# Two-block hybrid kernel: NSA loop pieces 8/6/5/5, compression in paired rows, 128x4 post-norm statistics

## The chip, the cores and the metric

One core of one Trainium2 chip runs the whole program. The metric is the time of one execution in device microseconds; the runs shown are three executions of the same kernel. An engine's name is short here: PE is TensorE, DVE is VectorE, ACT is ScalarE, POOL is GpSimd, SP is SyncE.

## What is computed

The reference runs two layers, one after the other, on one sequence of 512 tokens with 1024 channels, in fp32. Only what the change touches is told in detail.

- **First block.** RMS norm, an input projection `h @ w_in`, then NSA attention (8 query heads in 2 groups, head width 64), an RWKV-7 scan, a gated merge, an output projection and a convolutional FFN, each with a residual.
- Within NSA three attentions share the queries: one over compressed keys, one over selected blocks, one over a window. **Compression** takes blocks of 32 rows of 64 channels at a stride of 16 (31 blocks), adds a position term and multiplies by `w1`:

```python
blocks = z.reshape(B, S, G, Dh)[:, tok] + pe[None, None, :, None, :]
hid = jax.nn.silu(jnp.einsum('bnlgd,lde->bnge', blocks, w1))
return jnp.einsum('bnge,ef->bgnf', hid, w2)
```

- **Second block.** SwiGLU FFN, a mixer (dilated-window attention and a chunkwise mLSTM, with sigmoid gates), and a second SwiGLU FFN. Each of the three results goes through an RMS norm of its own before it is added to `x`; these are the three **post norms**:

```python
x = x + 0.5 * rmsnorm(f, ffn1_post_g[l])
x = x + rmsnorm(y, mix_post_g[l])
x = x + 0.5 * rmsnorm(f, ffn2_post_g[l])
```

- The mLSTM needs running sums and running maxima of its input and forget gates over time, one row of 512 per head (`b = cumsum(log f)`, and the running maximum of `i - b`).

## The kernel before

Activations lie with channels on the 128 partitions and the 512 tokens along the free axis. A **unit** is one 128-column block of a weight matrix against all 1024 channels: eight k-steps. fp32 weights and activations are split into a rounded high part and a low rest, so a unit is 24 matmuls of 128x512: high by high and low by high (`mm_hi`, 16), then high by low part of the weights (`mm_lo`, 8). All of them are recorded at L379, and `unit` is the helper that issues them. For each unit SP loads `raw` (512 KB), ACT rounds it to `w_hi` (`high_part`, L1117) as soon as the unit two before has been used, POOL makes `w_lo` in two instructions (L352), PE works, and DVE takes the PSUM bank out with the norm factor (`take`, L1599). Weights and the two PSUM banks of the units alternate between two slots. The order of the work on every engine is written out by hand; engines meet in counted semaphores.

**Compression** (PE L460 to 467). DVE adds the position term into `blocks` in four instructions of 128x496 (L1654), two for keys (`c` = 0, from `u[4]`) and two for values (`c` = 1, from `u[5]`), with the takes of units 6 and 7 between them. PE then runs, for 32 rows `l`, 2 tensors and 2 groups, a matmul with 64 contracted rows, 64 weight columns and 31 moving columns; both groups have their own bank (`p7`, `p6`). fp32 matmuls show up as two instructions each. ACT applies Silu in four instructions (L1170, L1172). Unit 8 follows on PE. The weights `cmp_w1` come by one DMA of 2 MB, written twice, once for either half of the partitions.

**The NSA loop** (PE from L621, 16 turns). Turn `t` handles query block `b = t % 4` of head pair `t // 4`, and its attention grows with `b`: the scores are 128(b+1) wide. On PE a turn is `nsa_turn(t, 0)` (transposes of the exponentiated scores of group 0), `loop_part`, `nsa_back(t-1)` (transpose of the last turn's output, which waits for `nsa_mix`), `nsa_turn(t, 1)`, `nsa_scores(t+1)`, `loop_part`, `nsa_pv(t)` (128x65 matmuls). `nsa_turn(t, 1)` waits until ACT and DVE (`slc_copy`, `win_copy`, L1220 and L1764) have emptied the banks of group 0. The two `loop_part` calls of a turn carry one dense unit of the RWKV and merge projection, four k-steps each, in bank `p0`. Three units stand in four turns; the turn with `t % 4 == 0` has none:

```python
if t % 4 == 0:
    return
w = loop_unit(t)
```

DVE's turn is `win_copy` twice, `nsa_max(t+1)` (L1748), the take of the unit (L1805), `nsa_mix(t)` (L1771 to L1778, waits for `nsa_pv(t)`) and `mix_previous(t-1)` (L1788). ACT's is `slc_copy`, `nsa_store`, `slc_copy`, `nsa_exp(t+1)`, the `high_part` of the unit two ahead, `scale_part`.

**Post norms.** `f_tiles` (L2150) squares and sums eight tiles into `acc` (128x512). `stat_of_acc` (L430) sums over the partitions with an all-ones 128x128 weight into `p2`, so every partition holds all 512 sums; `stat_root` (L1127) takes the square root on 128x512; DVE takes the reciprocal in place in `p3` (L1615); `post_scale` (L2169) multiplies the eight stored tiles by `p3`, POOL (or DVE, in every other tile of the last norm) adds them to `x` and the next stage begins. This stands behind `down2`, `out2` and `down3`.

**Gate rows of the mLSTM.** DVE computes them on 4x512: `gate_sums` (L2199 to L2205, with a scan) behind column block 2, and `gate_maxima` (L2210 to L2214, with a scan) behind column block 3 of attention head 0. Column blocks 0 to 5 of a head are also rotated on DVE (`rope_it`, L2236 to L2247), and block 8 is the last before the attention steps, in which `att_max` (L2255) is DVE's next work.

## Time and profile before

| what | us |
|---|---|
| three runs | 2529.43, 2523.91, 2526.45 |
| median | 2526.45 |
| the profiled execution | 2526.31 |
| its span, first to last instruction | 2524.4 |
| mean granted TensorE clock, share of full speed | 0.974 |
| busy: PE / DVE / ACT / POOL | 2410.1 / 1050.1 / 959.8 / 1045.0 |

A unit has 24 matmuls; where PE has nothing else to do units follow each other every 5.44 us. In the chain of work that ended last PE has 86% of the span and DVE 9%. PE's busy time overlaps itself in places (a matmul's end is modelled), so it says when PE had no work, not how well it worked. In a timeline a row holds several equal instructions in a row (x8), its length is from the first start to the last end, and the bracket tells how long the engine had been idle and who ended that. "issue" is idle time with no releaser in the profile.

### The profile page before, as it was taken

The page shows a single profiled execution, that of the slowest core. Times are in us where ns is not written, and L with a number is a line of the kernel's source. Part 1 is how long each engine was busy: PE and PEld are TensorE (multiplying, and loading weights), DVE is VectorE, ACT ScalarE, POOL GpSimd, SP SyncE. Part 2 cuts the span into 40 slices and gives each one's busy share as a digit, 9 for nine tenths or more (in the row PEclk, how much of TensorE's full clock was granted, in tenths as well). Part 3 has the DMA queues.
Part 4 walks back from the last instruction along what each step waited for, and adds up shares of the span by engine and source line. Part 5 has one row for each costly group of instructions (what it writes and reads, how often), then busy time and mean ns, then how long its engine had stood idle before and what let it go on. Part 6 is the DMA issues. An engine that isn't in the chain of part 4 may idle for free.

```text
span 2524.4 us, 38784 instructions
## 1 busy us (share of the span) xinstructions
PE 2410.1 (95%) x13928; PEld 1953.1 (77%) x13928; DVE 1050.1 (42%) x1776; ACT 959.8 (38%) x1273; POOL 1045.0 (41%) x756
## 2 busy tenths in 40 slices
PE   8999998889999999999999799999999998999997
PEld 6877777767788888788887578787888775888885
DVE  3355464555555532322211856663333345322213
ACT  3244432233566643444422422223444523444321
POOL 4212230014445555555555533442433255455554
PEclk9899999989999999999999899999999998999998
DMA  4111120013232233222332212221222132223232
GB/s 171 58 42 38 46 71 16 3 42 110 82 100 99 92 101 107 92 95 96 100 100 100 96 59 76 84 78 65 76 82 78 64 100 67 85 98 100 93 107 83
DMA packets 56746, 205.24 MB, mean 81 GB/s; under 512 B 6828, under 2 KB 7596, under 8 KB 56268
## 3 DMA queue, kind: packets, MB, share of 16 engines
q1 hardware_dynamic: 55152, 196.45, 23.6%
q10 hardware_dynamic: 1504, 7.49, 0.8%
q8 instruction: 70, 1.15, 0.2%
q14 instruction: 20, 0.16, 0.0%
HBM read 201.81 MB, written 2.10 MB: 81 GB/s over the span
## 4 chain that ended last, share of the span: by engine, by line
PE 86%; DVE 9%; ACT 2%; issue 2%; POOL 0%; DMA 0%; DVEq 0%; ACTq 0%; SPq 0%
PE psum L379 84%; DVE rope_t L2245 2%; DVE qk_st L2244 1%; PE psum L554 1%; DVE rope_t L2237 1%; DVE qk_st L2247 1%; POOL x L364 0%; PE psum L978 0%; DVE psum L1615 0%; ACT w_hi L1117 0%; DVE inv L1934 0%; DVE o_acc L1778 0%; DVE rst L1615 0%; DVE soft_r L1773 0%; DVE tmp L2169 0%
## 5 line engine op out<-in xcount | busy, mean ns | idle before, releaser
L352 POOL TENSOR_TENSOR w_lo<-raw,w_hi 128x512 fp32r<-128x512 f32 x732 | 1014.6, 1407 | 1447.8 <-ACT w_hi L1117 1447.8
L379 PE MATMUL psum<-h_hi,w_hi 128*128 128x512 f32 x2192 | 890.6, 406 | 40.8 <-DVE h_lo L1621 26.0
L379 PE MATMUL psum<-h_lo,w_hi 128*128 128x512 f32 x2192 | 865.4, 395 | 0.0
L1117 ACT ACTIVATE w_hi<-raw 128x1024 fp32r<-128x1024 f32 x366 | 386.2, 1056 | 807.7 <-PE psum L379 796.8
L379 PE MATMUL psum<-h_hi,w_lo 128*128 128x512 f32 x2192 | 551.9, 391 | 0.0
L379 PEld LDWEIGHTS psum<-h_hi,w_hi 128*128 128x128 f32 x2192 | 419.0, 191 | 153.1 <-issue 54.2
L379 PEld LDWEIGHTS psum<-h_lo,w_hi 128*128 128x128 f32 x2192 | 419.5, 191 | 89.3 <-issue 6.9
L379 PEld LDWEIGHTS psum<-h_hi,w_lo 128*128 128x128 f32 x2192 | 412.8, 188 | 87.5 <-issue 1.4
L379 PE MATMUL psum<-hid_hi,w_hi 128*128 128x512 f32 x528 | 208.7, 395 | 0.0
L379 PE MATMUL psum<-hid_lo,w_hi 128*128 128x512 f32 x528 | 208.6, 395 | 0.0
L1599 DVE TENSOR_TENSOR tmp<-psum,rst 128x512 f32<-128x512 f32 x100 | 69.1, 691 | 319.5 <-PE psum L379 319.0
L379 PE MATMUL psum<-hid_hi,w_lo 128*128 128x512 f32 x528 | 134.9, 395 | 0.0
L2159 DVE TENSOR_TENSOR acc<-acc,sq 128x512 f32<-128x512 f32 x24 | 30.8, 1283 | 242.7 <-ACT sq L1403 242.7
L379 PEld LDWEIGHTS psum<-hid_hi,w_hi 128*128 128x128 f32 x528 | 99.1, 188 | 24.3 <-DVE tmp L2132 0.2
L379 PEld LDWEIGHTS psum<-hid_lo,w_hi 128*128 128x128 f32 x528 | 99.2, 188 | 24.0
L379 PEld LDWEIGHTS psum<-hid_hi,w_lo 128*128 128x128 f32 x528 | 99.1, 188 | 24.0
L2143 DVE TENSOR_TENSOR hid_lo<-tmp,hid_hi 128x512 f32 x66 | 50.9, 771 | 62.5 <-ACT hid_hi L1452 62.5
L1448 ACT ACTIVATE tmp<-tmp 128x512 f32<-128x512 f32 x44 | 27.8, 632 | 113.7 <-DVE tmp L1599 113.7
L1452 ACT ACTIVATE hid_hi<-tmp 128x512 f32 x66 | 41.7, 632 | 72.4 <-DVE tmp L2141 72.4
L2128 DVE SCALAR_TENSOR_TENSOR tmp<-psum,par,tmp 128x511 f32<-128x511 f32 x44 | 33.0, 750 | 71.1 <-ACT tmp L1440 71.1
L1448 ACT ACT_TABLE_LOAD x44 | 56.5, 1283 | 0.8
L1604 DVE TENSOR_TENSOR psum<-psum,rst 128x512 f32<-128x512 f32 x60 | 41.6, 694 | 35.6 <-PE psum L379 35.4
(391 smaller groups left out, 2533.5 us busy)
## 6 DMA issues: line engine op xcount, KB each, us to landing
raw<-in_w SPq DMA_DIRECT2D x366, 512.0 KB, 3.3
x<-in_x SPq DMA_DIRECT2D x4, 512.0 KB, 6.3
tmp<-in_cmp_w ACTq DMA_DIRECT2D x1, 2048.0 KB, 7.3
x<-in_x ACTq DMA_DIRECT2D x1, 2048.0 KB, 7.7
out_y<-x SPq DMA_DIRECT2D x8, 256.0 KB, 2.1
mask<-in_mask ACTq DMA_DIRECT2D x1, 1536.0 KB
masks<-in_masks ACTq DMA_DIRECT2D x1, 768.0 KB, 9.4
lora<-in_lora ACTq DMA_DIRECT2D x1, 512.0 KB, 3.7
```

The lines of the kernel that those rows point to most:

```text
L352: pool.tensor_tensor(w_lo[:, g.slot, part], raw[:, g.slot, part], w_hi[:, g.slot, part].bitcast(F32), ALU.subtract).then_inc(sem("lo_ready ...
L379: return pe.matmul(out, lhsT, rhs, start=start, stop=stop)
L554: last = pe.transpose(psum[:, 6 + r, tok(m)], att_s[t % 2][2 * g + r][:, tok(m)], ident[:])
L1117: act.activation(w_hi[:, g.slot], raw[:, g.slot], ACT.Copy).then_inc(sem("hi_ready"), 1)
L1448: act.activation(tmp[:, 2], tmp[:, 4], ACT.Silu).then_inc(sem("silu_done"), 1)
L1452: act.activation(tile_of(hid_hi, i), tmp[:, 3], ACT.Copy).then_inc(sem("hid_rounded"), 1)
L1599: dve.tensor_tensor(dst, psum[:, o.slot], rst[:], ALU.mult).then_inc(sem(f"freed{o.slot}"), 1)
L1604: dve.tensor_tensor(psum[:, o.slot], psum[:, o.slot], rst[:], ALU.mult)\
L2128: dve.scalar_tensor_tensor(tmp[:, c, 1:], psum[:, ob.slot, 0:T - 1], col("ffn_conv", 2 * KF + c + 2 * i), tmp[:, c, 1:], ALU.mult, ALU.add ...
L2143: dve.tensor_tensor(tile_of(hid_lo, i), tmp[:, 3], tile_of(hid_hi, i).bitcast(F32), ALU.subtract)\
L2159: dve.tensor_tensor(acc[:], acc[:], sq[:, ob.slot], ALU.add).then_inc(sem("acc_done"), 1)
L2245: dve.tensor_tensor(t, t, sin, ALU.mult).then_inc(sem("rope_a"), 1)
```

## The change

- **NSA loop.** Pieces of units no longer follow `t`: the four turns of a group carry 8, 6, 5 and 5 k-steps (all of unit 0 in turn 0; 3 and 3 k-steps of unit 1 in turn 1; the last 2 of unit 1 and the first 3 of unit 2 in turn 2; 3 and 2 of unit 2 in turn 3). Units end in turns 0, 2 and 3; the take on DVE and `high_part` on ACT follow them, in turn 2 the take stands between the two `win_copy`.
- **Compression.** Two rows (`l` even and odd) lie on the two halves of the partitions, and both groups side by side as moving columns. PE: 16 x 2 matmuls with 128 contracted rows, 64 weight columns and 62 moving columns into one bank. DVE: 16 additions of 64x248 in place of 4 of 128x496, eight before the take of unit 6 and eight behind it; the take of unit 7 now follows `blocks_ready`. ACT: three Silu. The weights come in two DMAs of 64 partitions, 1 MB in all, in runs of 64 elements.
- **Post norms.** PE multiplies `acc` as weights by one column of ones, four times, into 128x4 (token by partition); ACT's root and DVE's reciprocal work on 128x4; PE spreads the result with four matmuls against `ident` into `p3`.
- **Gate rows.** `gate_sums` goes behind column block 8 of head 0, `gate_maxima` behind that of head 1, the rest (`gate_floor`) behind that of head 2; the exponential on ACT moves from head 1 to head 3. `b_row` has another place in memory.

The diff, cut to what matters:

```diff
-        def loop_unit(t):
-            return Index(A_UNITS + 4 + 3 * (t // 4) + t % 4 - 1)
+        LOOP_PIECES = (((0, 0, 4), (0, 4, 8)), ((1, 0, 3), (1, 3, 6)), ((1, 6, 8), (2, 0, 3)), ((2, 3, 6), (2, 6, 8)))
+        def loop_unit(t, n):
+            return Index(A_UNITS + 4 + 3 * (t // 4) + n)
+        def unit_ended(t):
+            return (0, None, 1, 2)[t % 4]
...
+            def post_stat(a, r):
+                pe.wait_ge(sem("acc_done"), 9 * a + 9)
+                for b in range(TB):
+                    last = mm(p2[:, b:b + 1], acc[:, tok(b)], sel[:, 2:3])
+                last.then_inc(sem("stat_sum"), 1)
+                pe.wait_ge(sem("stat_rstd"), r + 1)
+                for b in range(TB):
+                    last = mm(p3[:, tok(b)], stat4[:, 1, b:b + 1].to_broadcast([128, 128]), ident[:])
+                last.then_inc(sem("stat_spread"), 1)
...
-            for l in range(32):
+            for l in range(16):
                 for c in range(2):
-                    for g in range(NG):
-                        last = mm((p7, p6)[g][half(c), 0:NC], cmp_w1[half(g), c, l],
-                                  blocks[half(g), c, l, 0:NC], l == 0, l == 31)
+                    last = mm(hidden[half(c)], cmp_w1[:, c, l], row_pairs[:, c, l], l == 0, l == 15)
...
-            def loop_part(t, ks):
-                if t % 4 == 0:
-                    return
-                w = loop_unit(t)
+            def loop_part(t, piece):
+                n, first, end = LOOP_PIECES[t % 4][piece]
+                w, ks = loop_unit(t, n), range(first, end)
...
+            def post_root(r):
+                act.wait_ge(sem("stat_sum"), r + 1)
+                act.activation(stat4[:, 0], p2[:, 0:TB], ACT.Sqrt, bias=eps, scale=1.0 / D).then_inc(sem("stat_root"), 1)
...
-            act.dma_start(cmp_w1, io["cmp_w1"]).then_inc(sem("cmp_in"), 16)
+            for n in range(2):
+                act.dma_start(cmp_w1[half(n)], io["cmp_w1"][half(n)].rearrange("p c (l n) e -> p c n l e", n=2)[:, :, n])\
+                    .then_inc(sem("cmp_in"), 16)
...
-                if t % 4:
-                    high_part(loop_unit(t) + 2)
+                if t % 4 != 1:
+                    high_part(loop_unit(t, unit_ended(t)) + 2)
...
+            def post_rstd(r, n):
+                dve.wait_ge(sem("stat_root"), r + 1)
+                dve.reciprocal(stat4[:, 1], stat4[:, 0]).then_inc(sem("stat_rstd"), 1)
+                dve.wait_ge(sem("stat_spread"), n)
...
             for c in range(2):
-                src = u[:, 4 + c].rearrange("p (n s) -> p s n", s=16)
-                for m in range(2):
-                    last = dve.tensor_tensor(
-                        blocks[:, c, 16 * m:16 * m + 16, 0:NC], src[:, :, m:m + NC],
-                        cmp_pe[:, c, 16 * m:16 * m + 16].unsqueeze(2).to_broadcast([128, 16, NC]), ALU.add)
-                    if m == 0:
-                        take_u(6 + c)
+                src = u[:, 4 + c].rearrange("p (n l a) -> p a l n", l=8, a=2)
+                add = cmp_pe[:, c].rearrange("p (l a) -> p a l", a=2)
+                for a in range(2):
+                    for g in range(NG):
+                        for m in range(2):
+                            last = dve.tensor_tensor(
+                                row_pairs[half(a), c, 8 * m:8 * m + 8, g], src[half(g), a, :, m:m + NC],
+                                add[half(g), a, 8 * m:8 * m + 8].unsqueeze(2).to_broadcast([64, 8, NC]), ALU.add)
+                if c == 0:
+                    take_u(6)
             last.then_inc(sem("blocks_ready"), 1)
+            take_u(7)
...
             for t in range(16):
                 win_copy(t, 0)
+                if t % 4 == 2:
+                    take_loop(t)
                 win_copy(t, 1)
...
-                        if hh == 0 and c == 2:
-                            gate_sums()
-                        if hh == 0 and c == 3:
-                            gate_maxima()
                         if c == 7:
                             att_max(0)
+                        if c == 8 and hh < 3:
+                            (gate_sums, gate_maxima, gate_floor)[hh]()
```

## Rows read from the trace of the kernel before

**Rows 1.** The page: engines over the whole span (busy us, share, instructions)
```profile
PE 2410.1 (95%) x13928; PEld 1953.1 (77%) x13928; DVE 1050.1 (42%) x1776; ACT 959.8 (38%) x1273; POOL 1045.0 (41%) x756
```

**Rows 2.** Windows of the NSA loop: stretch, length, busy (x instructions), clock, DMA
```profile
135.20:173.70 38.50, 36.51 (x228) 29.63 (x229) 20.56 (x72) 18.15 (x33) 8.68 (x7) 1.00 0.12 42
173.70:216.50 42.80, 39.94 (x231) 31.85 (x230) 24.35 (x79) 19.06 (x35) 7.54 (x7) 0.92 0.11 38
216.50:302.60 86.10, 81.32 (x450) 65.09 (x449) 44.97 (x148) 35.82 (x65) 16.11 (x13) 0.88 0.11 37
```

**Rows 3.** Windows around turn 0 of the second group
```profile
173.60:181.80 8.20, 5.94 (x28) 4.43 (x28) 5.57 (x25) 3.12 (x8) 0.43 (x1) 0.70 0.19 65
176.60:183.90 7.30, 6.93 (x27) 5.50 (x27) 4.50 (x19) 3.23 (x7) 0.00 (x0) 0.53 0.04 16
```

**Rows 4.** Timeline of PE in turn 2, second group: start, length, instruction, idle before
```profile
192.67 0.48 PE L379 MATMUL psum<-h_hi,w_hi 128*128 128x512 f32 x1
...
196.19 0.85 PE L554 MATMUL psum<-ident,tmp 128*128 128x128 f32 x6 [0.43 <-DVE blocks L1764]
```

**Rows 5.** Timeline of DVE in the same turn
```profile
192.29 0.18 DVE L1771 RECIPROCAL soft_r<-psum 128x4 f32<-128x4 f32 x1 [1.04 <-PE psum L379]
192.51 1.29 DVE L1773 TENSOR_TENSOR soft_r<-soft_r,gate_tm 128x4 f32<-128x4 f32 x1
...
195.51 0.54 DVE L1764 COPY blocks<-psum 128x384 f32<-128x384 f32 x1
```

**Rows 6.** Windows over the compression matmuls and the unit behind them
```profile
63.90:70.70 6.80, 6.76 (x256) 6.76 (x256) 1.00 (x1) 1.22 (x1) 2.20 (x2) 0.53 0.31 96
70.70:78.30 7.60, 7.60 (x29) 6.13 (x27) 0.00 (x0) 0.70 (x4) 0.00 (x0) 0.75 0.01 2
```

**Rows 7.** By tile: DVE's additions into `blocks`, duration ns min/median/max
```profile
L1654 DVE TENSOR_TENSOR blocks<-u,cmp_pe x4: 993/1022/2001, 52.1 to 62.8; 128x496 f32<-128x496 f32 x4
```

**Rows 8.** Timelines of POOL, DVE and PE around them
```profile
52.51 3.01 POOL L352 TENSOR_TENSOR w_lo<-raw,w_hi 128x512 fp32r<-128x512 f32 x2 [2.90 <-ACT w_hi L1117]
...
57.36 2.94 DVE L1654 TENSOR_TENSOR blocks<-u,cmp_pe 128x496 f32<-128x496 f32 x2
...
57.95 3.46 POOL L352 TENSOR_TENSOR w_lo<-raw,w_hi 128x512 fp32r<-128x512 f32 x2 [2.43 <-ACT w_hi L1117]
...
63.94 6.86 PE L379 MATMUL psum<-blocks,tmp 64*64 64x31 f32 x256 [1.78 <-DVE blocks L1654]
```

**Rows 9.** Timeline of PE: fp32 matmuls of other shapes
```profile
111.21 1.97 PE L379 MATMUL psum<-ident,rq 128*64 128x128 f32 x32
...
1481.19 1.50 PE L379 MATMUL psum<-v_tm,att_pT 128*128 128x129 f32 x12
```

**Rows 10.** Timeline behind the last down-projection tile of the first SwiGLU FFN
```profile
1391.18 1.20 PE L379 MATMUL psum<-acc,sel 128*128 128x512 f32 x2 [3.04 <-DVE acc L2159]
1392.42 0.66 ACT L1127 ACTIVATE psum<-psum,sel 128x512 f32<-128x512 f32 x1 [1.39 <-PE psum L379]
...
1393.11 3.37 DVE L1615 RECIPROCAL psum<-psum 128x512 f32<-128x512 f32 x1 [1.32 <-ACT psum L1127]
...
1396.51 1.88 DVE L2169 TENSOR_TENSOR tmp<-tmp,psum 128x512 f32<-128x512 f32 x3
```

**Rows 11.** Timeline of ACT: a small square root
```profile
81.99 0.29 ACT L1178 ACTIVATE rq<-psum,sel 128x32 f32<-128x32 f32 x1 [0.73 <-PE psum L379]
```

**Rows 12.** Attention head 0: timelines of DVE and PE
```profile
1439.06 2.19 DVE L2202 TENSOR_TENSOR_SCAN tmp<-tmp 4x512 f32<-4x512 f32 x1
...
1477.98 0.69 DVE L2255 CUSTOM_DVE_ANT_0 att_p<-psum,mask 128x512 f32<-128x512 f32 x1 [2.64 <-issue]
...
1443.64 0.47 PE L379 MATMUL psum<-h_hi,w_hi 128*128 128x512 f32 x1 [0.76 <-DVE qk_st L1599]
...
1453.63 0.77 PE L379 MATMUL psum<-h_hi,w_hi 128*128 128x512 f32 x1 [4.30 <-DVE qk_st L2283]
```

**Rows 13.** Window of the unit behind PE's longest wait there
```profile
1453.60:1460.90 7.30, 7.27 (x25) 5.95 (x26) 6.86 (x11) 0.00 (x0) 0.00 (x0) 0.77 0.22 74
```

More of the change, by code:

```diff
@@ L250, in build_program @@
         selh = sb("selh", [4, 128], scope=ml)
-        rows, b_row, zero_row = tmp[0:4, 0:4], tmp[0:4, 6], tmp[0:4, 7]
+        rows, b_row, zero_row = tmp[0:4, 0:4], mo[0:4, 4], tmp[0:4, 7]
         c_row, em_row, nmu_row = mo[0:4, 5], mo[0:4, 6], mo[0:4, 7]
@@ L605, in _ @@
                 nsa_turn(t, 0)
-                loop_part(t, range(0, 4))
+                loop_part(t, 0)
                 if t:
@@ L611, in _ @@
                     nsa_scores(t + 1)
-                loop_part(t, range(4, 8))
+                loop_part(t, 1)
                 nsa_pv(t)
@@ L1104, in _ @@
                     unit(Index(FIRST["out2"] + c, i, 2), Index(254 + c, i, 2), y2_hi, y2_lo, ("y_ready", 8))
-            stat_of_acc(3)
+            post_stat(3, 5)
             ffn_mm(2, 6, "up3", "down3", 262)
-            stat_of_acc(4)
+            post_stat(4, 7)
         @block.scalar
@@ L1168, in _ @@
             act.wait_ge(sem("gain_ready"), 1)
-            for g, bank in enumerate((p7, p6)):
-                act.activation(hid_cmp[:, g, 0:NC], bank[half(0), 0:NC], ACT.Silu)
-            for g, bank in enumerate((p7, p6)):
+            act.activation(hid_cmp[:, :, 0:NC], hidden[half(0)], ACT.Silu)
+            for g in range(NG):
                 last = act.activation(hid_rep[half(1), g, :, 0:NC],
-                                      bank[half(1), 0:NC].unsqueeze(1).to_broadcast([64, 4, NC]), ACT.Silu)
+                                      hidden[half(1), g].unsqueeze(1).to_broadcast([64, 4, NC]), ACT.Silu)
             last.then_inc(sem("cmp_act"), 1)
@@ L1499, in _ @@
                         high_part(gu + c)
-                        if hh == 1 and c == 0:
+                        if hh == 3 and c == 0:
                             act.wait_ge(sem("row_v"), 6)
@@ L1610, in low_h, with rms_rstd @@
                     .then_inc(sem("h_ready"), 1)
-            def rms_rstd(r, dst=rst[:]):
+            def rms_rstd(r):
                 dve.wait_ge(sem("stat_root"), r + 1)
-                dve.reciprocal(dst, p3).then_inc(sem("stat_rstd"), 1)
+                dve.reciprocal(rst[:], p3).then_inc(sem("stat_rstd"), 1)
                 dve.wait_ge(sem("stat_rstd"), r + 1)
+            def post_rstd(r, n):
+                dve.wait_ge(sem("stat_root"), r + 1)
+                dve.reciprocal(stat4[:, 1], stat4[:, 0]).then_inc(sem("stat_rstd"), 1)
+                dve.wait_ge(sem("stat_spread"), n)
             def low_x(nset, gains, k):
@@ L1651, in _ @@
             for c in range(2):
-                src = u[:, 4 + c].rearrange("p (n s) -> p s n", s=16)
-                for m in range(2):
-                    last = dve.tensor_tensor(
-                        blocks[:, c, 16 * m:16 * m + 16, 0:NC], src[:, :, m:m + NC],
-                        cmp_pe[:, c, 16 * m:16 * m + 16].unsqueeze(2).to_broadcast([128, 16, NC]), ALU.add)
-                    if m == 0:
-                        take_u(6 + c)
+                src = u[:, 4 + c].rearrange("p (n l a) -> p a l n", l=8, a=2)
+                add = cmp_pe[:, c].rearrange("p (l a) -> p a l", a=2)
+                for a in range(2):
+                    for g in range(NG):
+                        for m in range(2):
[4 more added lines that the diff above has]
+                    take_u(6)
             last.then_inc(sem("blocks_ready"), 1)
+            take_u(7)
             dve.tensor_scalar(gain[:, 0:3], par[:, COL["qk_gain"] + 1:COL["qk_gain"] + 4],
@@ L1796, in _, with take_loop @@
             cmp_out(3)
+            def take_loop(t):
+                w = loop_unit(t, unit_ended(t))
+                dve.wait_ge(sem("unit_used"), w.value(1))
+                dve.tensor_tensor(zm[:, w.at - A_UNITS, 1:], p0, rst[:], ALU.mult).then_inc(sem(f"freed{w.slot}"), 1)
             for t in range(16):
                 win_copy(t, 0)
+                if t % 4 == 2:
+                    take_loop(t)
                 win_copy(t, 1)
```

29 lines of the change are left out of this document (15 added, 14 removed).

## The prediction

> **What bounds the kernel now.** I read the page first, then windows over the stages, then the timelines of PE and DVE where the change falls. PE has work in 95% of the span [rows 1], so only three things can give time back: PE's idle time, time at the lower of its two clock levels (1.2 instead of 2.4 GHz), and PE instructions that go away. For each edit the reader is to look for these three at its place. The profiled execution took 2526.3 us, its span is 2524.4; the sum below is made against 2526.3, and the median of the runs, 2526.45, is the same within 0.2 us.
>
> **NSA loop.** The loop is four groups of four turns. The first takes 38.5 us at granted clock 1.00 with PE busy 36.5 us; the second takes 42.8 at 0.92, the last two 86.1 at 0.88, so 128.9 for three, 43.0 each [rows 2]. The difference sits in turn 0, which has no dense piece: in 8.2 us around it PE is busy 5.94, so 2.3 us idle, and from there it runs 7.3 us at clock 0.53 [rows 3], which costs 7.3 x (1 - 0.53) = 3.4 us. Together 5.7 us. The change puts a whole unit, 8 k-steps, into that place, so both go. It adds two piece starts per group (8 pieces for 6, some 0.15 us each as PE's first matmul of a piece is longer, 0.48 against 0.39: 0.3 in all), hence work of 36.8 us.
>
> What is late next is DVE. Behind a turn's `nsa_pv` it must do `nsa_mix`, `mix_previous` and `win_copy` before PE may start the second transposes. In turn 2 of the second group this ran from 192.1 (DVE's wait ended at 192.29) to 196.19, 4.1 us, against which PE had a piece of four k-steps (12 matmuls, 2.7 us, from 192.67) and still waited 0.43 us [rows 4, 5]. Of the 4.1 us some 1.1 is one 4-column operation that took 1.29 us where the reciprocal of the same size took 0.18 [rows 5]; POOL is then at work on the unit just rounded. After the change that piece has 3, 2, 3 k-steps in turns 1, 2, 3, so 0.7, 1.4 and 0.7 us less cover; in turn 2 the stall goes (no unit ends in turn 1, POOL has nothing), and in turn 1 it comes (unit 0 now ends in turn 0). I take waits of 1.1, 0.7 and 0.5 us, and none in turn 0, where four k-steps lie before the transposes: 2.3 us a group. Bounds: 0.8 if POOL is never in the way, 4.0 if always. A group is then 36.8 + 2.3 = 39.1 us, and the three lose 128.9 - 117.3 = **11.6 us** (16.7 to 6.5). The first group, at full clock already, stays at its 38.5. The take in turn 2, now between the two copies, costs 0.7 us of DVE while PE has transposes and scores: nothing. The `high_part` on ACT behind turn 0 stands behind `nsa_exp`, and `slc_copy` of the next turn only has to be there a piece later: nothing. Each unit's weights are still rounded one whole unit ahead, and SP's loads move with them; POOL, which frees `raw` for them, is busy 41% [rows 1].
>
> **Compression.** PE: 256 instructions took 6.86 us at clock 0.53 [rows 6, 8], with four 64x64 tiles side by side; now 64 with two. An instruction of two tiles with 128 moving columns took 1.97/32 = 0.062 us at full clock [rows 9]; so 64 cost 3.9 us, or at most double, 7.9, if the clock is low, as it was in the unit behind a wait of 4.30 us [rows 12, 13] and will be after the wait below. With half the columns I take 5.8 us: 1.0 saved. The Trainium skill's "TensorEngine Tiling (Array Packing)", section Instruction Overhead, says that a matmul has an overhead of about 60 cycles and that one column costs as much as 60. By that page the rounds count, 64 before and 32 now, and 6.86 would become an estimated 3.4 us; no row here shows it.
>
> DVE: an addition of 496 columns took 0.99 us when alone and 2.00 when POOL was at work [rows 7, 8]; POOL's own pair, 2.5 us of work, took 3.01 and 3.46 beside them [rows 8]. So they take turns, whole instruction by whole instruction. An addition has now half the columns, 0.55 us, and there are 16: 8.8 us for 4.0 of before, on half the partitions each, so nothing is gained by their height. From 52.1: eight additions (4.4), the take of unit 6 (0.7), eight more (4.4) end at 61.8 with no wait, when PE finishes unit 7 (62.2); PE began at 63.94, so the gain would be 1.7. But each POOL pair that meets them puts two instructions of about 1.25 us between them. The pairs start at 52.5 and 57.95 [rows 8] and one unit, 5.4 us, later at 63.4; the first two push the end to about 66.8, so the third is met too, and it becomes 69.2. PE would start at 69.3, **5.4 us later**. The skill's "SBUF — State Buffer" (on the shared GPSIMD/Vector port) calls it an exclusive lock held for the whole instruction, not a split of bandwidth. By sharing instead of a lock the three pairs would cost half, some 3.7 us, and PE would start near 65.5; the 2.00 beside 0.99 speaks for the lock. I take the lock: +5.4 - 1.0 = **+4.4 us**, bounds -6.5 (no wait, 1.7; matmuls at 3.9 us, 3.0; no low clock in unit 8, which cost 7.6 x 0.25 = 1.9 [rows 6]) and +7. The take of unit 7 has 5 us until unit 9 needs its bank. Two DMAs in runs of 256 bytes are issued 27 us before they are needed; ACT's queue had over 3 us to spare before the next rounding. Nothing for both.
>
> **Post norms.** From the last sum into `acc` to the first scaling DVE, ACT and PE take 1391.18 to 1396.51: 5.3 us, of which PE 1.20, root 0.66, reciprocal 3.37 [rows 10]. Nothing covers it. New: eight fp32 instructions of 128x128 weights (0.125 us each [rows 9], 1.0), root 0.29 [rows 11], reciprocal 0.18 [rows 5], eight instructions at 0.125 (1.0) or, the clock having fallen, 2.0, and 0.4 for four hand-overs. That is 2.9 at full clock, 3.8 with the second eight slow, 4.9 with both. I take 3.8: 1.5 us, three times, **4.5 us** (1.2 to 7.2). POOL sets the pace behind it, but only starts with the first scaled tile, so all moves forward.
>
> **Gate rows.** In head 0 they stand in DVE's stream between the rotations, and PE waited 0.76 and 4.30 us for banks [rows 12]; the unit behind ran 7.3 us at clock 0.77, a loss of 1.7 [rows 13]. Heads 1 to 3 have the same rotations and no such wait. Behind block 8 DVE is idle 2.64 us before `att_max` [rows 12], and each third of the gate rows (about 2.9, 2.3, 1.7 us, the scan alone 2.19 beside POOL) fits within that to some tenths. 6.8 less 0.2 for each of three heads: **6.2 us** (4.5 to 7). If that cover were gone it would cost up to 2 us a head.
>
> **Sum:** -11.6 + 4.4 - 4.5 - 6.2 = -17.9, so 2508.4 us.
>
> **Rivals.**
> - *The clock still falls once in a group* (turns 2 and 3 have 5 k-steps where they had 8; small matmuls ran at 0.53 at 63.9 [rows 6]). It gives back 3.4 x 3 = 10.2: 2518.6. Against it: the first group stays at 1.00 through its turns 1 to 3, with 3.5 us of 128x65 matmuls in a row. 14%.
> - *The additions escape POOL, or the tiles run side by side at their best.* With no wait the compression gains 1.7 + 1.0 and the end is 2501.3; with all of the lower bound it gains 6.5: 2497.5. The packing of the tiling page above belongs here. For it: only one of four additions was slowed. Against: 16 in a row leave no gap. 22%.
> - *Slower: the thinner pieces let the clock fall in each of turns 1 to 3*, 3.4 us each, and DVE is always in POOL's way. A group is 36.8 + 4.0 + 10.2 = 51.0; 3 x 8.0 + 12.5 = 36.5 slower, less 6.3 for the rest: 2557. It needs 7 such falls in 16 turns to be slower by 0.2%. 3%.
> - *It does less than it says at each place*: the waits of a group are 4.0 us (6.5 gained), the compression costs 7, the post norms give 1.2 and the gate rows 4.5, since part of them delays `att_max`: 5.2 us in all, 2521, at the edge of 0.2% (5 us, about what a measurement of this kernel can tell from no change). 4%.
>
> **Numbers.** The forecast has 57%. The range 2498 to 2519 takes in the first two rivals and the bounds of the compression; the last two are left out. Faster by over 0.2%: 0.93; within: 0.04; slower: 0.03.
>
> **What would show it.** Right: all groups of the loop at clock 1.00 and 38 to 40 us; PE waiting for `win_copy` in turns 1 and 2; compression matmuls starting near 69 with an idle row of 5 to 7 us before them, released by DVE's additions; three chains of about 4 us behind the post norms; no wait of PE in head 0. Wrong: additions of 0.5 us without gaps, a group over 41 us, clock under 0.95 in the loop, or `att_max` waiting behind the gate rows.

## The result and the profile after

| what | before | after |
|---|---|---|
| median of the runs on one chip, us | 2526.53 (4 runs) | 2496.44 (4 runs, 2493.66 to 2503.9) |
| the profiled execution, us | 2526.31 | 2493.66 |
| its span, us | 2524.4 | 2491.6 |
| mean granted clock | 0.974 | 0.985 |

The ratio is 0.9885, with a 95% interval of 0.9861 to 0.991: 29 us less, 23 to 35. The forecast had 18 us less, 2508.4, and a range that began at 2498. A second measurement of the same kernel beside others (below) gave 0.9876 (0.9857 to 0.9894); one of its four executions took 11162.88 us and is left out. Here and below a time saved in us is one minus the ratio, times the time of the kernel before; the difference of the two medians can be up to 2 us off it. So the direction was right, and the size was too small by more than the range allowed.

The page of the kernel after, engines over the whole span; it answers to [rows 1]:

```profile
PE 2393.4 (96%) x13778; PEld 1943.3 (78%) x13778; DVE 1047.7 (42%) x1788; ACT 958.4 (38%) x1272; POOL 1048.5 (42%) x756
```

PE is busy 16.7 us less, and the span is 32.8 us shorter: the other half is idle time of PE. Now the four places.

**The NSA loop.** Windows over the first three of its four groups of four turns; they answer to [rows 2], and the last row to the first of [rows 3] (a stretch of 8.2 us that in either kernel lies about the seam of two groups). A row has the stretch, its length, the busy time of PE, of PE's weight loads, of DVE, ACT and POOL, then the granted clock, the busy share of the DMA engines and GB/s:

```profile
138.60:175.90 37.30, 36.37 (x227) 29.41 (x228) 20.07 (x72) 18.14 (x33) 7.88 (x7) 1.00 0.13 43
175.90:213.60 37.70, 36.75 (x230) 29.40 (x230) 23.28 (x79) 18.92 (x35) 8.46 (x7) 1.00 0.13 43
213.60:251.30 37.70, 36.73 (x230) 29.39 (x230) 23.29 (x79) 18.91 (x35) 8.47 (x7) 1.00 0.13 43
...
173.60:181.80 8.20, 8.20 (x54) 6.76 (x54) 4.15 (x15) 2.41 (x6) 2.51 (x2) 1.00 0.21 65
```

The clock is 1.00 in all of them and PE has no gap at the seam: 8.20 us busy of 8.20, where it had 5.94. A group is 37.7 us with 36.75 busy. The work was forecast at 36.8; the waits are 0.95 us, not 2.3. PE's waits in the second group, from its timeline:

```profile
195.96 0.85 PE L572 MATMUL psum<-ident,tmp 128*128 128x128 f32 x6 [0.55 <-DVE blocks L1797]
206.99 1.06 PE L572 MATMUL psum<-ident,tmp 128*128 128x128 f32 x8 [0.29 <-DVE blocks L1797]
```

These are turns 2 and 3, 0.55 and 0.29 against a forecast of 0.7 and 0.5. The wait of 1.1 forecast for turn 1 isn't there. DVE and POOL around it:

```profile
184.61 0.16 DVE L1806 TENSOR_TENSOR soft_r<-soft_r,gate_tm 128x4 f32<-128x4 f32 x1
184.81 0.99 DVE L1811 SCALAR_TENSOR_TENSOR o_acc<-psum,soft_r,o_acc 128x64 f32<-128x64 f32 x4
185.71 0.92 DVE L1821 SCALAR_TENSOR_TENSOR zm<-zm,par 128x512 f32<-128x512 f32 x1
...
184.78 2.98 POOL L361 TENSOR_TENSOR w_lo<-raw,w_hi 128x512 fp32r<-128x512 f32 x2 [7.75 <-ACT w_hi L1134]
```

The 4-column operation that took 1.29 us in [rows 5] takes 0.16: it ended 0.01 us before POOL's pair began. The pair lies beside the next two operations and costs them next to nothing: the four that read PSUM take 0.99 as in the turn without POOL, and `mix_previous` takes 0.92 instead of 0.74. From the loop's first matmul to the merge's first, 169.6 us have become 151.9. This part repeats: from the first to the last transpose of the turns (L554 before, L572 after) it is 144.8 us in each of the nine traces of kernels that have the new pieces, and 161.2 to 162.9 in the four that have the old ones without extra work.

**Compression.** Timelines of DVE and POOL, then of PE, over the additions; they answer to [rows 8]:

```profile
53.22 6.21 DVE L1686 TENSOR_TENSOR blocks<-u,cmp_pe 64x248 f32<-64x248 f32 x8
59.45 0.69 DVE L1622 TENSOR_TENSOR u<-psum,rst 128x512 f32<-128x512 f32 x1
60.06 7.47 DVE L1686 TENSOR_TENSOR blocks<-u,cmp_pe 64x248 f32<-64x248 f32 x8
...
53.60 2.79 POOL L361 TENSOR_TENSOR w_lo<-raw,w_hi 128x512 fp32r<-128x512 f32 x2 [2.90 <-ACT w_hi L1134]
59.04 2.99 POOL L361 TENSOR_TENSOR w_lo<-raw,w_hi 128x512 fp32r<-128x512 f32 x2 [2.65 <-ACT w_hi L1134]
64.47 2.70 POOL L361 TENSOR_TENSOR w_lo<-raw,w_hi 128x512 fp32r<-128x512 f32 x2 [2.45 <-ACT w_hi L1134]
...
67.67 3.68 PE L388 MATMUL psum<-blocks,tmp 128*64 128x62 f32 x64 [4.43 <-DVE blocks L1686]
71.28 0.79 PE L388 MATMUL psum<-h_hi,w_hi 128*128 128x512 f32 x1
```

As forecast, three POOL pairs meet the additions and PE waits longer, 4.43 us instead of 1.78. But the stall is smaller (5.0 us in all instead of 7.5), and the matmuls take 3.68 us instead of 6.86. The sixteen additions one by one (line view, ns min/median/max), beside [rows 7]:

```profile
L1686 DVE TENSOR_TENSOR blocks<-u,cmp_pe x16: 555/578/1556, 53.2 to 66.0; 64x248 f32<-64x248 f32 x16
```

Ten of them take 555 to 591 ns, where the next one starts some 0.54 us after the last. Five take 1460 to 1556 and a sixth 857: one for each of POOL's six instructions. An addition that POOL meets is up to 0.98 us longer; in [rows 7] it was 2001 instead of 993, 1.0 more: the same step, though POOL's instruction takes about 1.25 alone. (1556 against 578 agrees with the exclusive lock of the Trainium skill's "SBUF — State Buffer": a short addition and a long one are held up by the same 1.0 us, not slowed by a share.)

**Post norms.** Timeline behind `down2`; it answers to [rows 10]. Below it PE's rows of the middle norm and of the last:

```profile
1372.28 1.05 PE L388 MATMUL psum<-sel,acc 128*128 128x1 f32 x8 [3.04 <-DVE acc L2197]
1373.37 0.26 ACT L1149 ACTIVATE stat<-psum,sel 128x4 f32<-128x4 f32 x1 [1.25 <-PE psum L388]
...
1373.67 0.18 DVE L1644 RECIPROCAL stat<-stat 128x4 f32<-128x4 f32 x1 [0.78 <-ACT stat L1149]
1373.90 2.08 PE L388 MATMUL psum<-ident,stat 128*128 128x128 f32 x8 [0.57 <-DVE stat L1644]
...
1376.02 1.88 DVE L2207 TENSOR_TENSOR tmp<-tmp,psum 128x512 f32<-128x512 f32 x3 [2.17 <-PE psum L388]
...
2094.05 1.86 PE L388 MATMUL psum<-sel,acc 128*128 128x1 f32 x8 [3.04 <-DVE acc L2197]
2096.48 2.08 PE L388 MATMUL psum<-ident,stat 128*128 128x128 f32 x8 [0.57 <-DVE stat L1644]
...
2476.20 1.05 PE L388 MATMUL psum<-sel,acc 128*128 128x1 f32 x8 [1.50 <-DVE acc L2197]
...
2477.82 1.16 PE L388 MATMUL psum<-ident,stat 128*128 128x128 f32 x8 [0.57 <-DVE stat L1644]
```

From 1372.28 to 1376.02 it is 3.74 us (5.33 before), as the forecast's 3.8 with the second eight slow. In the middle norm both sets of eight are slow and the chain is 4.54 us (6.20 before). In the last norm the second eight run at full clock, 1.16 instead of 2.08, and its chain is 2.82 us (5.26 before). The clock at these places differs between executions: in the seven other traces with these norms and no extra work the first takes 3.18 to 4.55 us, the middle one 3.73 to 4.55 and the last 2.81 to 4.09.

**Gate rows.** PE's waits of 0.76 and 4.30 us among the column blocks of head 0 are gone. DVE behind block 8:

```profile
1446.22 1.10 DVE L2324 TENSOR_TENSOR tmp<-psum,rst 128x512 f32<-128x512 f32 x1 [4.19 <-PE psum L388]
1447.22 0.67 DVE L2237 SCALAR_TENSOR_TENSOR tmp<-tmp 4x512 f32<-4x512 f32 x1
1447.93 2.17 DVE L2240 TENSOR_TENSOR_SCAN mo<-tmp 4x512 f32<-4x512 f32 x1
1450.04 0.67 DVE L2296 CUSTOM_DVE_ANT_0 att_p<-psum,mask 128x512 f32<-128x512 f32 x1
```

`att_max` follows the scan without idle time. Between the first matmul behind the post norm and the first attention score, 7.6 us are gone.

**Where the 32.8 us of span went**, by the same landmarks in both traces: start-up +1.1; to the take of unit 8, -1.5; from there to the loop's first matmul +3.8; the loop -17.8; from there to the first post norm -4.5; the norm -1.6; attention head 0 -7.6; from there to the end of `down3` -2.2, the second norm in it; the last norm -2.4. Of these, +3.8 and -4.5 lie in code that the change doesn't touch, and +1.1 is within what start-up varies: in four traces of kernels with the old compression its matmuls begin at 63.86, 63.94, 64.73 and 65.31. The +3.8 can be seen: windows of the same 343 PE instructions behind unit 8, first the kernel after and then the kernel before:

```profile
77.80:138.60 60.80, 59.76 (x343) 50.02 (x341) 21.84 (x47) 16.77 (x23) 16.64 (x14) 0.86 0.16 53
```

```profile
78.20:135.20 57.00, 55.23 (x343) 46.20 (x341) 22.30 (x47) 16.76 (x23) 16.61 (x14) 0.94 0.17 56
```

Clock 0.86 against 0.94. In a second execution of the kernel after, the same code ran at 0.97:

```profile
77.00:132.00 55.00, 53.22 (x338) 44.44 (x337) 21.93 (x47) 16.43 (x23) 16.65 (x14) 0.97 0.17 58
```

So this stretch swings by nearly 6 us between executions of one program. The one behind the loop swings too: from the last transpose of the turns to the first matmul of the first norm's sum, the fourteen traces have 358.1 to 366.9 us for code that no run changes, and even the kernel after alone has 358.1 and 362.3. A single pair of traces doesn't show effects of a few us in either. That is why the experiments below were timed in five rounds.

### The profile page after: what moved, and what is told of

Same layout as the page of the kernel before. It is cut to its first block, busy times and chain, and to the rows that moved or that the text cites. A ratio compares the mean times of both kernels' runs of the same rounds, so it can differ in the third digit from the quotient of the medians.

```text
span 2491.6 us, 38495 instructions
## 1 busy us (share of the span) xinstructions
PE 2393.4 (96%) x13778; PEld 1943.3 (78%) x13778; DVE 1047.7 (42%) x1788; ACT 958.4 (38%) x1272; POOL 1048.5 (42%) x756
## 4 chain that ended last, share of the span: by engine, by line
PE 87%; DVE 9%; issue 2%; ACT 2%; DMA 0%; POOL 0%; DVEq 0%; ACTq 0%; SPq 0%
PE psum L388 85%; DVE rope_t L2286 2%; DVE qk_st L2285 2%; DVE rope_t L2278 1%; DVE qk_st L2288 1%; PE psum L572 1%; DVE blocks L1686 1%; PE psum L995 0%; DVE o_acc L1811 0%; ACT w_hi L1134 0%; DVE inv L1972 0%; DVE rst L1638 0%; DVE tmp L2207 0%; ACT zm L1394 0%; PE psum L685 0%
## 5 line engine op out<-in xcount | busy, mean ns | idle before, releaser
L2179 DVE TENSOR_TENSOR tmp<-tmp 128x512 f32<-128x512 f32 x66 | 52.4, 795 | 8.1
```

Source lines behind the costliest of these rows:

```text
L2179: dve.tensor_tensor(tmp[:, 3], tmp[:, 2], tmp[:, 1], ALU.mult).then_inc(sem("gated"), 1)
```

## The experiments

Twelve kernels ran, in three series of four, each series beside the kernel before on one chip (the second series on another chip than the rest). First each part of the change alone, put into the kernel before.

**The loop alone.** The edit is `LOOP_PIECES` with its `loop_part`, `take_loop` and `high_part` places:

```diff
+        LOOP_PIECES = (((0, 0, 4), (0, 4, 8)), ((1, 0, 3), (1, 3, 6)), ((1, 6, 8), (2, 0, 3)), ((2, 3, 6), (2, 6, 8)))
-                loop_part(t, range(0, 4))
+                loop_part(t, 0)
```

> The kernel before with only the NSA loop's pieces changed. Theory A (read from the two traces: every group of four turns goes from 43.0 to 37.7 us at full clock, the first from 38.4 to 37.3): 17 us faster than before, granted clock 1.00 in all groups, about 1 us of waits of PE left in a group. Rival B (the prediction's term): 11.6 us faster, 2.3 us of waits left in a group. Rival C (the gain in the loop partly came from where the compression left the clock): under 10 us.

Measured: 2511.03 (2506.05 to 2514.57) against 2531.45, ratio 0.9916 (0.9898 to 0.9934): 21.3 us less, 16.7 to 25.8. The forecast's 11.6 lies outside, its upper bound of 16.7 at the edge. In the trace the loop is as long as in the kernel after: Theory A. Rivals B and C are out.

**The compression alone.**

```diff
-            for l in range(32):
+            for l in range(16):
                 for c in range(2):
-                    for g in range(NG):
-                        last = mm((p7, p6)[g][half(c), 0:NC], cmp_w1[half(g), c, l],
-                                  blocks[half(g), c, l, 0:NC], l == 0, l == 31)
+                    last = mm(hidden[half(c)], cmp_w1[:, c, l], row_pairs[:, c, l], l == 0, l == 15)
```

> The kernel before with only the compression in paired rows. Theory A (traces: matmuls 3.7 us later relative to the takes less 1.1 us of start, then 3.7 instead of 6.9 us, unit 8 about 1.2 us shorter): between 3 us faster and 2 us slower, so no difference beyond 0.2%. Rival B (prediction): 4.4 us slower, since the additions wait for POOL. In the trace both expect PE to wait 3 to 5 us for DVE's additions.

Measured: 2526.58, ratio 0.9986 (0.9972 to 1.0001): 3.5 us less, between 7 less and 0.3 more. The forecast's 4.4 more (Rival B) is excluded; Theory A's 3 less to 2 more holds. Its PE row is that of the whole change:

```profile
67.69 3.68 PE L381 MATMUL psum<-blocks,tmp 128*64 128x62 f32 x64 [4.44 <-DVE blocks L1658]
```

**The post norms alone.**

```diff
-            stat_of_acc(2)
+            post_stat(2, 3)
```

> The kernel before with only the three 128x4 post-norm statistics. Theory A and the prediction's term agree within a microsecond: the chain from the last sum into acc to the first scaling goes from 5.3 to 3.7 us where PE is slow in the second half and to 2.8 us where it is not, so 4.5 to 6.5 us faster in all. Rival: POOL's additions set the pace and take it back, under 2 us.

Measured: 2523.4, ratio 0.9972 (0.9959 to 0.9984): 7.1 us less (4 to 10). The forecast had 4.5, bounds 1.2 to 7.2; the rival's under 2 is out.

**The gate rows alone.**

```diff
-                        if hh == 0 and c == 2:
-                            gate_sums()
-                        if hh == 0 and c == 3:
-                            gate_maxima()
+                        if c == 8 and hh < 3:
+                            (gate_sums, gate_maxima, gate_floor)[hh]()
```

> The kernel before with only the gate rows moved behind column block 8 of heads 0 to 2. Theory A: 6.8 us faster (the waits of 0.76 and 4.30 us and 1.7 us of low clock), up to 7.6, and PE never waits in head 0. Rival B: part comes back because att_max starts later in heads 0 to 2: 4.5 us or less.

Measured: 2523.65, ratio 0.9974 (0.996 to 0.9989): 6.6 us less (3 to 10), forecast 6.2. The interval takes in both theories. In the trace the two waits of PE among the column blocks of head 0 are gone, from the first norm's sum to the first `att_max` it is 7.0 us less than in the kernel before, and from there to the second norm's sum 0.3 more: Theory A.

The four sum to 38.5 us against 29 to 31 for the whole; with their intervals of 3 to 5 us each the difference isn't one that needs a cause. The second series looks at the two terms that were off.

**The kernel after, again.**

> The changed kernel as it is, as the base for the others of this call. All theories: 28 to 38 us faster than before (ratio 0.985 to 0.989). If the four parts add up as they measured alone (21.3, 3.5, 7.1, 6.6 us): 38 us; if the first measurement holds: 29 us.

Measured: 2495.46, 2497.1 and 2498.07, ratio 0.9876 (0.9857 to 0.9894), 31.4 us less.

**The kernel after with the old compression** (the edit above, reversed).

> The changed kernel with the compression of before (four additions, 128 matmuls of 64 rows). Theory A (pairing rows is worth about 3 us): 1 to 5 us slower than the changed kernel. Rival B (prediction: the additions cost more than the matmuls give): 4 us faster than it.

Measured: 2498.1 (2496.25 to 2504.31), ratio 0.9875 (0.9859 to 0.9891). By the ratio there is no difference, by the medians it is 1.0 us slower; Rival B's 4 us faster doesn't show. But each interval is some 4 us wide to either side, so this pair alone refutes neither theory. The two estimates of the term, here and from the compression alone, are 0 and 3.5 us less.

**Unit 8 ahead of the compression matmuls.** The kernel after, with one line moved, so that PE has 5.4 us of dense work where it waited 4.43 us for DVE:

```diff
             for c in range(1, 8):
                 nsa_unit(c)
 
+            nsa_unit(8)
             pe.wait_ge(sem("cmp_in"), 64)
...
             last.then_inc(sem("cmp_mm"), 1)
-            nsa_unit(8)
```

> The changed kernel with unit 8 issued on PE before the compression matmuls. Theory A (PE's wait of 4.4 us for DVE's additions is real and on the path, and the low clock of unit 8 comes from it): 5 to 7 us faster than the changed kernel, with a wait under 0.5 us before the matmuls. Rival B (the low clock comes from the small matmuls and only moves on to unit 9): 3.5 to 4.5 us faster.

Measured: 2489.46 (2481.73 to 2494.85), ratio 0.9836 (0.982 to 0.9852): 41.5 us under the kernel before, and by the medians 7.6 under the kernel after; its slowest run is faster than the fastest of the kernel after beside it (2495.46), though not than the fastest on record (2493.66). That is more than either theory said. The wait is gone and the matmuls run at full clock, as Theory A has it:

```profile
68.90 2.08 PE L388 MATMUL psum<-blocks,tmp 128*64 128x62 f32 x64
70.91 4.55 PE L388 MATMUL psum<-sel,zm 128*128 128x2 f32 x32
```

But the lower clock begins at 73.6, 2.6 us behind the compression matmuls and among the 32 matmuls of 2 columns, so part of Rival B holds in this execution: a low stretch followed, only later.

**The kernel before with extra work in turn 0.** Eight matmuls of 128x512 in each turn with `t % 4 == 0`, four in either place where the loop has no piece. They use weights and inputs at hand, and their sums go unread: the next unit starts its bank afresh.

```diff
             def loop_part(t, ks):
 
                 if t % 4 == 0:
+                    w = loop_unit(t + 1)
...
+                    for k in ks[:2]:
+                        mm(p0, w_hi[:, w.slot, tok(k)], h_hi[:, k])
+                        mm(p0, w_hi[:, w.slot, tok(k)], h_lo[:, k])
                     return
```

> The kernel before with eight extra 128x512 matmuls in every turn of the NSA loop that has no dense piece (four ahead of the second transposes, four behind the scores), into the free bank p0, their result unused: more work, the same waits. It is to tell the clock's part of the loop's gain from the waits' part. Theory A (turn 0's waits and small matmuls alone let the clock fall; 3.4 us a group are the clock's): clock 0.98 to 1.00 in all groups, groups 2 to 4 at 40 to 40.8 us, 6 to 9 us faster than before. Rival B (the clock would fall anyway, filler or not): groups of 43 to 44 us, no gain or 1 to 4 us slower.

Measured: 2521.63 (2516.03 to 2523.16), ratio 0.9964 (0.995 to 0.9978): 9.1 us less than the kernel before (5.6 to 12.6; 8.0 by the medians), with more work. From the first to the last transpose of the turns it has 153.3 us where the kernel before has 161.2. That is Theory A. Windows of two groups, beside [rows 2]:

```profile
148.10:188.80 40.70, 38.82 (x237) 31.02 (x236) 24.44 (x79) 19.07 (x35) 7.59 (x6) 1.00 0.12 40
188.80:229.60 40.80, 38.92 (x238) 31.02 (x237) 24.44 (x79) 19.07 (x35) 7.58 (x6) 1.00 0.12 39
```

The groups fall from some 43 to 40.75 us, and the clock stays at 1.00. In [rows 2] the last three groups have PE busy (39.94 + 81.32) / 3 = 40.4 us each and idle 2.5. Here it is busy 38.9, of which the eight extra matmuls at 0.227 us are 1.8, so the old instructions take 37.1: 3.3 us less for the same work, while PE still idles 1.9 us. That is the clock's part of a group, which the forecast put at 3.4. The run doesn't tell whether it was the idle time in turn 0 or the lack of dense matmuls there that let the clock fall: the extra ones shorten one wait (1.27 to 0.34 us) and stand among the small ones, too.

The third series takes the compression apart: a wait for DVE, the clock behind it, and the number of matmuls.

**Old rows, unit 8 first.** The kernel with unit 8 first, with the compression of before in it.

> The kernel after, with unit 8 of the NSA part ahead of the compression matmuls, and with the old rows again (256 matmuls of 64x64 tiles, four additions of 496 columns). PE then meets no wait before the compression matmuls, and the matmuls run at full clock. Theory A (the pairing pays nothing even where its wait is hidden: the old 256 matmuls are issued four to a round and at full clock take some 3.5 to 4 us, half of their 6.9): at most 2 us slower than the kernel with unit 8 first and paired rows, so 2490 to 2492. Theory B (the pairing halves the compression at any clock, and the wait for its many additions hid that): the old matmuls take about 5.4 to 6.9 us against 2.1, so 3.5 to 5 us slower, 2493 to 2495.

Measured: 2495.29 (2491.23 to 2499.34), ratio 0.9862 (0.9841 to 0.9883), 5.4 us over its neighbour with paired rows (next run), as Theory B has it. By five runs of each the difference is uncertain by some 4 us, so it is the rows of PE that decide:

```profile
68.03 3.80 PE L386 MATMUL psum<-blocks,tmp 64*64 64x31 f32 x242
73.22 0.43 PE L386 MATMUL psum<-blocks,tmp 64*64 64x31 f32 x14 [1.39 <-issue]
```

At full clock the old 256 instructions take 5.6 us from first to last: 15.7 ns each, and near their end PE stands still for 1.39 us while the profile shows nothing that it waited for. Of the 3.5 us over the 2.1 of the paired rows, 1.4 are this pause and 2.1 the number of matmuls. The clock behind it was 0.62 for 8.4 us, as this window shows:

```profile
73.60:82.00 8.40, 8.40 (x42) 7.72 (x41) 0.62 (x3) 3.85 (x8) 2.49 (x2) 0.62 0.19 64
```

**Unit 8 first, again.**

> The kernel after with unit 8 ahead of the compression matmuls, once more, as the measure for its neighbours. Theory A (the wait of 4.4 us goes, the matmuls take 2.1 instead of 3.7 us, and unit 8 runs at full clock, which gives 1.0): 7.0 us less than the kernel after, so 2490.5 against 2497.5. Theory B (the 8 us seen were the clock's luck in the first 140 us, which moves the start of the loop by up to 7 us between executions of one program): 2494 to 2497.

Measured: 2489.86 (2487.75 to 2493.41), ratio 0.9842 (0.9823 to 0.9862). That is Theory A's number, and it repeats the first run of this kernel within 0.4 us. Its matmuls take 2.0 us, to the next instruction:

```profile
68.41 2.08 PE L388 MATMUL psum<-blocks,tmp 128*64 128x62 f32 x64
70.42 3.73 PE L388 MATMUL psum<-sel,zm 128*128 128x2 f32 x32
```

**The kernel after, its wait filled.** Unit 8 stays behind the matmuls:

```diff
+            for b in range(18):
+                mm(p6, h_hi[:, 0, 0:128], h_hi[:, 1])
             pe.wait_ge(sem("cmp_in"), 64)
             pe.wait_ge(sem("blocks_ready"), 1)
```

> The kernel after, with 18 extra matmuls of 128x512 (0.227 us each, 4.1 us; their results go unread into a free bank) where PE waits 4.43 us for the additions. The wait stays, only PE isn't idle in it. Theory A (the gain of moving unit 8 is 4.4 us of wait and 2.6 us of clock): the clock stays at 1.00, the matmuls take 2.1 us instead of 3.7, unit 8 takes 5.4 instead of 6.4, and the kernel is 2 to 3 us faster than after: 2495. Theory B (it is all wait, and the clock falls at the compression matmuls anyway, since they are small): the same as after, 2497.5, or slower by some tenths.

Measured: 2495.53 (2491.69 to 2497.17), ratio 0.9863 (0.9844 to 0.9882). By time alone it can't be told from the kernel after (0.9876), though it lies where Theory A has it. The trace tells them apart:

```profile
63.79 4.24 PE L388 MATMUL psum<-h_hi 128*128 128x512 f32 x18
68.46 2.08 PE L388 MATMUL psum<-blocks,tmp 128*64 128x62 f32 x64 [0.43 <-DVE blocks L1688]
70.47 0.50 PE L388 MATMUL psum<-h_hi,w_hi 128*128 128x512 f32 x1
...
76.05 3.63 PE L388 MATMUL psum<-sel,zm 128*128 128x2 f32 x32
```

The same 64 instructions in 2.08 us instead of 3.68, and unit 8 in 5.6 us (70.47 to 76.05) instead of 6.4. From the first compression matmul to the end of unit 8 it is 7.6 us; the kernel after has 10.0. So at this place it isn't the small matmuls that bring the clock down, but PE's idle time before them. (In all three traces with this wait of 4.43 us the matmuls ran at 0.50, in all four where it is filled or gone at 1.00.)

**Post norms with PE kept busy**, on top of unit 8 first. Ten extra matmuls ahead of the wait for the last sum and two between the two sets of eight:

```diff
+                for b in range(10):
+                    mm(p5, h_hi[:, 0, 0:128], h_hi[:, 1])
                 pe.wait_ge(sem("acc_done"), 9 * a + 9)
...
+                for b in range(2):
+                    mm(p5, h_hi[:, 0, 0:128], h_hi[:, 1])
                 pe.wait_ge(sem("stat_rstd"), r + 1)
```

> The kernel after with unit 8 ahead of the compression matmuls, and in each post norm 10 extra matmuls of 128x512 ahead of the wait for the last sum (PE is idle 3.0 us there) and 2 between the two sets of eight (idle 0.57 us); their results go unread into a free bank. Theory A (the second eight took 2.08 us at the lower clock and 1.16 at full clock, by PE's idle time before them): chains of 2.8 to 3.0 us in all three norms instead of 3.7, so 1.5 to 2 us faster than with unit 8 first alone. Theory B (the lower clock comes from the small matmuls themselves, and the extra ones only stand in the way): no faster, or up to 1 us slower.

Measured: 2489.43 (2488.08 to 2492.46), ratio 0.9841 (0.9822 to 0.986), 0.4 us under its neighbour: no difference that the runs can tell. The first norm in the trace:

```profile
1369.18 1.05 PE L388 MATMUL psum<-sel,acc 128*128 128x1 f32 x8 [0.79 <-DVE acc L2201]
1370.09 0.71 PE L388 MATMUL psum<-h_hi 128*128 128x512 f32 x2
1370.80 1.39 PE L388 MATMUL psum<-ident,stat 128*128 128x128 f32 x8
...
1372.22 1.88 DVE L2211 TENSOR_TENSOR tmp<-tmp,psum 128x512 f32<-128x512 f32 x3 [1.48 <-PE psum L388]
```

The second eight take 1.39 us instead of 2.08, and the chain is 3.04 us; it was 3.74 in the kernel after and 4.55 in the neighbour's trace, where both sets were slow. In the middle norm both sets now run at full clock, and the chain is 2.81 us instead of 4.55:

```profile
2092.08 1.05 PE L388 MATMUL psum<-sel,acc 128*128 128x1 f32 x8 [0.80 <-DVE acc L2201]
...
2093.70 1.16 PE L388 MATMUL psum<-ident,stat 128*128 128x128 f32 x8
```

In the last norm it is 2.71 instead of 2.82, at full clock already. So Theory A's chains came in all three norms, 3.4 us shorter together than in the neighbour's trace, whose span is 3.1 us longer. The gain of 1.5 to 2 us isn't shown by the timing: the medians lie 0.4 us apart, and the five runs of each spread over 4 to 6 us.

## Why the forecast was too small

The places and the mechanisms were right, and the sizes of two terms failed: the waits left in a group of the loop, and the compression, whose stall and matmuls were both put too high, so that it came out as a loss. Each makes up some 6 us of the 11 to 13 that were missing.

**Bound and places.** That PE sets the time, and that only idle time, low clock and fewer instructions pay, held: PE's busy time fell by 16.7 us and its idle time by the rest. All four parts acted where they were said to.

**The loop: forecast -11.6, timed -21.3 (16.7 to 25.8), in the traces -17.8.** The mechanism held, and so did the work of a group, 36.8 forecast and 36.75 measured. Two terms were mis-sized. The waits: 2.3 us forecast, 0.95 measured. Of the 1.35 us too many, nearly all is the 1.1 put on turn 1, from the 1.29 us of one 4-column operation in [rows 5]. What was taken for the cost of POOL being at work was the cost of one operation beginning while POOL was in the middle of an instruction. In turn 1 that operation ends just before POOL's pair begins, and the operations beside the pair lose some 0.2 us together. Three groups then give 15.8 (128.9 less 3 times 37.7) instead of 11.6. And the first group was held at its 38.5 us as "at full clock already"; but it had PE idle 2.0 us too, and is now 37.3 with 0.9 idle, so 1.2 less. The rest, 0.8 us, came at the loop's end. (The bound of 16.7 us is a slip: with waits of 0.8 us a group is 37.6, and 128.9 less 3 times 37.6 is 16.1. The measured loop lies beyond it.) That the clock's 3.4 us per group come back with the idle time gone was right, and the kernel before with extra work shows it by itself.

**Compression: forecast +4.4, timed 0 and -3.5, in the traces -1.5.** This is the term with the wrong sign. "5.4 us later" was 2.6 by the landmarks (3.73 later, of which 1.09 is start-up), since the three POOL pairs held the additions up for 5.0 us and not 7.5. All six of POOL's instructions were met, as forecast, but a hit costs at most 0.98 us, not POOL's whole 1.25, and one of the six cost only 0.28. (The chain without stalls, from 52.1, adds up to 61.6 and not 61.8.) The number 1.0 stood in [rows 7] (2001 less 993) and wasn't used. And "5.8 us" for the matmuls was 3.68, though the clock was low as forecast: I had taken the 0.062 us of an instruction with 128 moving columns, with some off for half the columns. Measured are 57.5 ns at the low clock and 32.5 at full clock, against 26.8 and 15.7 for the old 64x64 ones. Per round of tiles that lie side by side, that is 115 and 65 ns for 62 columns (two tiles) and 107 and 63 for 31 columns (four tiles): a round costs the same with twice the columns. That agrees with the overhead per matmul in the Trainium skill's "TensorEngine Tiling (Array Packing)", section Instruction Overhead, and the estimate of 3.4 us worked out from it was near the 3.68; the sum went by the rows instead, and the runs decide for the page. The stretch of low clock behind it was shorter, too: unit 8 took 6.4 us instead of 7.4, a term that the forecast held at nothing and named only in a bound. So PE began 2.6 us later, and 3.1 us in the matmuls and 1.0 in unit 8 came back.

**Post norms: forecast -4.5, timed -7.1 (4 to 10).** The first norm took 3.74 us where 3.8 was forecast; that it came so close is in part luck, since other executions have 3.18 to 4.55. The middle one took 4.54 and not 3.8, but the forecast had put it at 5.3 before, and it was 6.20. The last took 2.82 and not 3.8, because the clock was still at the upper level there. In the traces the three give some 5.7. This lies within the bounds.

**Gate rows: forecast -6.2, timed -6.6, in the traces -7.6.** Each of its three pieces held (the two waits, the slow unit behind them, a cover that just suffices).

**The sum.** By terms: the loop added 6 us to what was forecast, the compression 6, the post norms 1, the gate rows 1. That is 14 more than 18, so 32, and the runs have 29 to 31. The result lies near the 2497.5 of the rival "additions escape POOL, tiles pack best", but not for its reason: the additions didn't escape, the matmuls packed, and nearly half of the surplus came from the loop. The rival on the slower side, a clock that falls in the thinner pieces, is refuted: the clock is 1.00 throughout the loop. So is the one that it falls once in a group.

**What the compression is worth.** The third series shows that the pairing is good for 3.5 us in the trace (5.6 against 2.1 us at full clock, 1.4 of it the pause) and 5.4 in the timing, once PE doesn't wait for DVE. As it was put in, the longer chain of additions (16 for 4) took that back through the wait. With unit 8 ahead, the wait (4.4), the slow matmuls (1.6) and the slow start of unit 8 (0.8 to 1.0) go at once: 7 us forecast from rows, 7.6 measured between the medians. This version, 2489.5 to 2489.9 us, is faster than both kernels.

**Left open.** Why the same code between unit 8 and the loop runs at a mean clock of 0.86 in one execution and 0.97 in another isn't settled. PE's waits don't explain it: up to the 1.12 us just before the loop, which both have, the slower execution has none and the faster one has one of 0.71 us. The lower level can show as early as the 32 matmuls of 2 columns behind the compression, which took 4.55 us in one execution of the kernel with unit 8 first and 3.73 in the other. A wait of PE isn't always followed by it, either: ahead of the old compression PE waits 1.8 us in six traces, and in five of them the clock falls in the matmuls behind it, but in that of the post norms alone they run at full clock (63.86 to 69.26, 5.4 us with a pause of 1.2). Nor is what PE stands still for in the midst of the 256 small matmuls (0.7 to 1.4 us in six of seven traces, none in the 64).

## What to carry to other kernels

Price a piece of idle time on PE by what it does to the clock behind it, too: in this kernel 1.6 us of idle time less per group of the loop, with the dense work moved into its place, gave 5.3 us, and 4.4 us less before the compression gave 7 to 8. Where a chain of small operations on another engine gets longer, first look for a dense piece that can be moved ahead of PE's wait; here one moved line was worth more than the edit it followed. And a stall taken from one row (1.29 us, where the same operation takes 0.16 alone) belongs to the moment at which it fell, so ask in the new order which operation begins while the other engine is in mid-instruction, before adding it to each turn.

## What the runs showed of the hardware

- Two tiles of 128x64 with 62 moving columns cost per round what four of 64x64 with 31 cost: 65 and 63 ns at the upper clock level, 115 and 107 at the lower.
- A DVE operation on SBUF that met a POOL instruction of 1.25 us was up to 0.98 us longer, whether it took 0.58 or 0.99 us alone, and less where it began late in POOL's (0.18 to 0.51). One of 4 columns that began 0.02 us behind POOL's ended 0.02 us behind it, 1.29 us instead of 0.16. Four operations that read one operand from PSUM beside the same pairs were not longer (0.99 us for four, with POOL and without).
- The granted clock didn't fall for 64 small matmuls in a row (2.08 us) when dense ones ran up to them; with 4.43 us of idle time before them they ran at 0.50 throughout. Where they had run at full clock, the clock fell 2.6 to 12.2 us behind them.
- A row of 256 small matmuls held a pause of 0.7 to 1.4 us without a wait in six of seven executions; 64 of double size had none.
